# A per-layer gate stage with its weight tiles outside four rows, and the fourth norm's last rows in pairs

## The chip, the cores and the metric

The program runs on one core of a Trainium2 chip. The metric is the time of one execution in device microseconds (us); the median of the runs counts. The engines are TensorE (PE, with its weight loads as PEld), VectorE (DVE), ScalarE (ACT), GpSimd (POOL), and SyncE (SP), which only issues DMAs. Each works through its own instruction stream in order and waits on semaphores that the others raise.

## What is computed

Two transformer blocks run on a sequence of 1024 tokens of width 1024, in float32. The stage of this change is the end of the first block: a feed-forward part, then a gate computed from the normed x that scales a projection of a second input p (1024 x 256), and then the final norm, whose result is the second block's x. The second block begins with a norm of its own and with gates from `w_in_2`.

```python
x = x + jnp.square(jax.nn.relu(h @ w_ffn_up[i])) @ w_ffn_down[i]
ple_gate = jax.nn.sigmoid(rmsnorm(x, g_ple[i]) @ w_ple_gate[i])
x = x + ple_gate * (p[i] @ w_ple_proj[i])
...
x = rmsnorm(x, g_final)                  # "x2", kept for the second block's residual
h = rms_norm(x, g_mix_2); gates = sigmoid((h @ w_in_2)[..., gate columns] + b_gate_2)
```

## The kernel before

**Tiles and products.** Tokens lie in eight rows t = 0..7 of 128; rows 0-3 are half 0, rows 4-7 half 1. Every large product is made in float32 precision from halves: a value is split into a high part (ACT, a copy with rounding) and a low part (a subtraction), and `three` issues three matmuls per 128-deep slice. A weight tile is two slices of 128 x 512. It goes from HBM into one of three stage buffers (SP), ACT makes its high part (L398), and POOL (L406) or DVE (L414) its low part; in the per-layer stage the two take turns. A ring holds five split tiles. `o.released()` after a tile's last use puts the conversion of the tile five further on into the order at that place; its DMA was issued when the tile three before it was done.

**Order.** `order_*` functions write one list of steps by hand, and each engine runs its own part of every step in that order. A step that stands earlier in the list stands earlier in the queue of each engine that has a part in it. `handover` is a barrier for all engines but PE: each waits for the last signal that the others raised before it.

**Norm.** `norm(nid)` is a generator that the stages advance. For each four rows: `rstd` (small DVE operations around a square root on ACT), then per row `scale_rows` on DVE (L523), `turn` on PE (eight 128 x 128 transposes, L534), its high part on ACT (L544) and low part on DVE (L555). Two buffers `xn` hold scaled rows. Norm 3 feeds the per-layer gate, norm 4 the second block; both write the transposed `hT`.

**Last feed-forward group** (`order_ffn`, end). For t = 0..7 the two halves n = 0, 1 of a row are multiplied (6 matmuls each), added to x on DVE (L2045) and squared on ACT (L1903). From row 3 on, norm 3 of half 0 is advanced by one step a row. At row 7 each tile is released right after its last matmuls, ahead of that row's squares and of turn 3.

**Per-layer stage** (`order_first_half`). After the handover p (1 MB) and `w_ple_proj` (1 MB) are loaded. For each half and each n, four weight tiles are taken. A row's gate is 24 matmuls in a row through all four tiles (`pe_ple_gate`). It needs the turned rows of the whole half. Then come the projection (`pe_ple_proj`, four plain float32 matmuls, L2139), sigmoid on ACT (L2148), product and sum on DVE (L2162, L2165) and a square on ACT (L1903). All eight transposes-by-four of p (`p_turn`, L2102) stand after the first row's gate. At the fourth row all four tiles are released at once, ahead of that row's sigmoid. The x2 norm runs in pairs of rows (`order_rows`: root, scaling L2062, four squares L2073 on ACT). Norm 4 of half 0 is advanced in the second half.

**Start of the second block** (`order_lru`). Four gate tiles are used on half 0 each and then on half 1 each. `staggered` puts norm 4's step for rows 4-7 first, turn 4 after the third gate, turn 5 after the fourth, then turns 6 and 7.

**PSUM.** `K.open(key)` gives the eight banks in a ring ("all") and waits until the bank's last holder has been read.

Of the kernel before, what the change touches and what calls it, by code (L numbers as in the profile page):

```python
# [256 lines left out]
class Kernel:  # L257
# [26 lines left out]
    def restart(self):  # L284
        for s in self.signals():
            s.n = 0
        for q in (self.pe, self.a, self.v, self.g, self.sp):
            q.seen, q.latest = {}, None
        self.ring_at = {"all": 0, "work": 0}
        self.holder = {}  # L290
# [7 lines left out]
    def open(self, key, ring="all"):  # L298
# [4 lines left out]
        elif ring == "work":  # L303
            banks = (3 + self.ring_at["work"] % 4,)
            self.ring_at["work"] += 1
        else:
            banks = ring
# [44 lines left out]
    def need_hT(self, nid, half):  # L352
        self.pe.wait_ge(self.S.hT_hi, (nid, half))
        self.pe.wait_ge(self.S.hT_lo, (nid, half))

# [194 lines left out]
def dve_turn(K, nid, t):  # L550
    v, n = K.v, K.norms[nid]
    for k0 in range(0, ND, 4):
# [3 lines left out]
                          ALU.subtract).then_inc(*K.S.hT_lo.up((nid, t // (NT // 2))))  # L556
        K.free(("turn", nid, t, k0), K.S.hT_lo)
# [1532 lines left out]
def sp_ple_load(K):  # L2090
    io, S = K.io, K.S
    K.sp.q.dma_start(K.prow[:, :, :], io["p"][0, 0].rearrange("(t p) c -> p t c", p=P)).then_inc(*S.p_load.up("p", 16))
    K.sp.q.dma_start(K.wpp[:, :, :], io["w_ple_proj"][0].rearrange("(k p) n -> p k n", p=P)).then_inc(*S.p_load.up("p", 16))

def pe_p_turn(K):
    for c in range(2):
        for t0 in range(0, NT, 4):
            b = K.open(("pT", c, t0))
            K.pe.wait_ge(K.S.p_load, "p")  # L2100
            for t in range(4):
                mm = K.pe.q.transpose(b[:, t * P:(t + 1) * P], K.prow[:, t0 + t, c * P:(c + 1) * P], K.ident[:, :])  # L2102
            mm.then_inc(*K.S.mm.up(("pT", c, t0)))

def dve_p_turn(K):
    v, S = K.v, K.S
    for c in range(2):
        for t0 in range(0, NT, 4):
            v.wait_ge(S.mm, ("pT", c, t0))  # L2110
            v.q.tensor_copy(K.pT[:, c, t0 * P:(t0 + 4) * P], K.bank(("pT", c, t0))).then_inc(*S.dve_evac.up(("pT", c, t0)))
            K.free(("pT", c, t0), S.dve_evac)

def pe_ple_gate(K, t, n, w0):
    pe, S, key = K.pe, K.S, ("ple", t, n)
    tc, hT = slice(t * P, (t + 1) * P), K.norms[3]["hT"]
    b = K.open(key)
    K.need_hT(3, t // (NT // 2))
    k = 0  # L2120
    for w in range(w0, w0 + 4):
        K.need_weight(w)
        hi, lo = K.weight(w)
        for i in range(2):
            mm = three(pe.q, b, (hT[0][:, k, tc], hT[1][:, k, tc]), (hi[:, i, :], lo[:, i, :]), k == 0, k == ND - 1)
            k += 1
        if w == w0 + 3:
            mm.then_inc(*S.mm.up(key))
            K.tile_done(w)
        elif t % (NT // 2) == NT // 2 - 1:  # L2130
            mm.then_inc(*S.mm.up(("tile", w)))

def pe_ple_proj(K, t, n):
    b = K.open(("pp", t, n))
    K.pe.wait_ge(K.S.dve_evac, ("pT", 1, 4))
    K.pe.wait_ge(K.S.p_load, "p")
    for k in range(2):
        mm = K.pe.q.matmul(b, K.pT[:, k, t * P:(t + 1) * P], K.wpp[:, k, n * HALF:(n + 1) * HALF], start=k == 0, stop=k == 1)  # L2139
# [337 lines left out]
def lay_out(K):  # L2477
# [71 lines left out]
    for i in (1, 2):  # L2549
# [15 lines left out]
    K.act = {1: pair("act", [P, 4, S])}  # L2565
    m.lo = above_x
# [5 lines left out]
    K.pT, K.prow, K.wpp = put("pT", [P, 2, S]), put("prow", [P, NT, PLE]), put("wpp", [P, 2, D])  # L2572
# [26 lines left out]
        4: {"to": K.gain, "row": io["g_mix_2"][0], "after": (3, NT - 1)},  # L2599
# [91 lines left out]
class Order:  # L2691
# [33 lines left out]
    def norm(self, nid):  # L2725
        for half in range(NHALF):
            ts = range(half * NT // 2, (half + 1) * NT // 2)
# [361 lines left out]
def order_ffn(o, f, norm, last_group, block_done):  # L3089
# [3 lines left out]
    for kind, i in ffn_plan(blocks):  # L3093
# [31 lines left out]
def order_first_half(o):  # L3125
    io = o.io
    norm = order_merge(o, 1, 2, [(io["w_o_mla"][0], NR, False), (io["w_o_rwkv"][0], NR, True)], io["w_out"][0])
    ple_norm = o.norm(3)
# [270 lines left out]
```

## Time and profile before

| | us |
|---|---|
| median of 3 runs (3667.73 to 3674.22) | 3673.79 |
| the profiled execution, its own time | 3660.88 |
| span of the profiled execution | 3659.5 |
| PE busy | 3488.4 (95%) |
| per-layer stage, from norm 3's turn of row 3 to the first gate of half 1 in the second block | 1949.68 to 2137.84 |

### The profile page before, as it was taken

To read this page: it belongs to the slowest core of one execution; us is meant where nothing else is said; L and a number is where in the kernel's file an instruction comes from. 1 tells how busy PE (TensorE), PEld (TensorE's weight loads), DVE (VectorE), ACT (ScalarE), POOL (GpSimd) and SP (SyncE) were. 2 spreads that over 40 slices of the span, in tenths; PEclk is the share of its full clock that TensorE was granted. 3 is DMA by queue.
4 is the path that set the end of the run, shared out by engine and by line. 5 is a ranking of instruction groups with operands and counts; after the bars stand their busy time and mean duration, and the time that the engine had idled before them with its cause. 6 is when DMAs were issued, how large, how long until landed. Compare 5 with 4: busy or idle time off the path is not lost.

```text
span 3659.5 us, 48530 instructions
## 1 busy us (share of the span) xinstructions
PE 3488.4 (95%) x20382; PEld 2834.9 (77%) x20382; DVE 1776.6 (49%) x2383; ACT 1291.5 (35%) x2197; POOL 1055.1 (29%) x592
## 2 busy tenths in 40 slices
PE   6999999999989999999998989999899999999998
PEld 5788887887668788888886667777687788888886
DVE  4563636426754433333335538984544434434435
ACT  4342333334543321211223547771232333223232
POOL 3221222110023233333331116762344223223221
PEclk9999999999999999999999999999899999999999
DMA  4111111010035311111112232223454311111111
GB/s 141 33 29 45 40 31 45 27 50 13 1 110 173 98 52 50 49 52 47 46 52 75 86 98 80 79 78 98 160 186 135 124 46 49 50 47 47 52 46 52
DMA packets 282377, 253.66 MB, mean 69 GB/s; under 512 B 11621, under 2 KB 221985, under 8 KB 282160
## 3 DMA queue, kind: packets, MB, share of 16 engines
q1 hardware_dynamic: 267552, 216.29, 19.4%
q10 hardware_dynamic: 11520, 25.17, 1.8%
q0 software_dynamic: 3088, 9.10, 0.7%
q8 instruction: 162, 2.65, 0.3%
q14 instruction: 55, 0.45, 0.0%
HBM read 213.81 MB, written 36.70 MB: 68 GB/s over the span
## 4 chain that ended last, share of the span: by engine, by line

## 5 line engine op out<-in xcount | busy, mean ns | idle before, releaser
L406 POOL TENSOR_TENSOR weight_lo<-stage,weight_hi 128x1024 fp32r<-128x1024 f32 (+4 forms) x265 | 625.8, 2366 | 1439.0 <-ACT weight_hi L398 1438.8
L369 PE MATMUL psum<-hT_hi,weight_hi 128*128 128x512 f32 x2240 | 891.0, 398 | 10.1 <-DVE hT_lo L555 7.4
L370 PE MATMUL psum<-hT_lo,weight_hi 128*128 128x512 f32 x2240 | 879.3, 393 | 0.0
L371 PE MATMUL psum<-hT_hi,weight_lo 128*128 128x512 f32 x2240 | 878.8, 392 | 0.0
L369 PEld LDWEIGHTS psum<-hT_hi,weight_hi 128*128 128x128 f32 x2240 | 425.8, 190 | 109.7 <-issue 11.8
L370 PEld LDWEIGHTS psum<-hT_lo,weight_hi 128*128 128x128 f32 x2240 | 425.6, 190 | 91.7 <-issue 4.3
L371 PEld LDWEIGHTS psum<-hT_hi,weight_lo 128*128 128x128 f32 x2240 | 425.0, 190 | 90.1
L398 ACT ACTIVATE weight_hi<-stage 128x1024 fp32r<-128x1024 f32 (+4 forms) x329 | 316.0, 975 | 464.5 <-PE psum L371 411.5
L2045 DVE TENSOR_TENSOR x<-x,psum 128x512 f32<-128x512 f32 x432 | 289.8, 686 | 215.4 <-PE psum L371 214.8
L369 PE MATMUL psum<-weight_hi,act_hi 128*128 128x512 f32 x864 | 339.0, 392 | 0.0
L371 PE MATMUL psum<-weight_hi,act_lo 128*128 128x512 f32 x864 | 338.7, 392 | 0.0
L370 PE MATMUL psum<-weight_lo,act_hi 128*128 128x512 f32 x864 | 338.7, 392 | 0.0
L2006 DVE SCALAR_TENSOR_TENSOR xn<-raw,param,xn 128x1024 f32<-128x1024 f32 x44 | 104.1, 2366 | 350.2 <-ACT xn L1991 350.2
L1943 DVE TENSOR_TENSOR rel<-rel,psum 128x512 f32<-128x512 f32 x64 | 44.0, 687 | 305.4 <-ACT rel L1932 305.4
L371 PEld LDWEIGHTS psum<-weight_hi,act_lo 128*128 128x128 f32 x864 | 162.4, 188 | 36.2
L370 PEld LDWEIGHTS psum<-weight_lo,act_hi 128*128 128x128 f32 x864 | 162.4, 188 | 36.0
L369 PEld LDWEIGHTS psum<-weight_hi,act_hi 128*128 128x128 f32 x864 | 162.4, 188 | 35.9
L414 DVE TENSOR_TENSOR weight_lo<-stage,weight_hi 128x1024 fp32r<-128x1024 f32 (+2 forms) x64 | 111.6, 1750 | 125.8 <-ACT weight_hi L398 122.1
L369 PE MATMUL psum<-br_hi,weight_hi 128*128 128x512 f32 x352 | 141.0, 401 | 19.2 <-POOL br_lo L1785 12.1
L1951 POOL TENSOR_TENSOR act_lo<-rel,act_hi 128x512 fp32r<-128x512 f32 x64 | 83.3, 1301 | 238.5 <-ACT act_hi L1936 238.5
L370 PE MATMUL psum<-br_lo,weight_hi 128*128 128x512 f32 x352 | 139.9, 397 | 0.0
L371 PE MATMUL psum<-br_hi,weight_lo 128*128 128x512 f32 x352 | 139.9, 397 | 0.0
(376 smaller groups left out, 5282.4 us busy)
## 6 DMA issues: line engine op xcount, KB each, us to landing
stage<-in_w_in SPq DMA_DIRECT2D x64, 512.0 KB, 4.0
stage<-in_w_up SPq DMA_DIRECT2D x44, 512.0 KB, 3.8
scratch_gates<-gate ACTq DMA_DIRECT2D x64, 256.0 KB, 2.0
gs<-scratch_gates SPq DMA_DIRECT2D x64, 256.0 KB, 2.8
stage<-in_w_out SPq DMA_DIRECT2D x32, 512.0 KB, 4.9
stage<-in_w_ffn_up SPq DMA_DIRECT2D x32, 512.0 KB, 4.2
stage<-in_w_ffn_down SPq DMA_DIRECT2D x32, 512.0 KB, 3.6
stage<-in_w_down SPq DMA_DIRECT2D x22, 512.0 KB, 3.5
```

The source lines that it names most:

```text
L369: q.matmul(out, stat[0], mov[0], start=first, stop=False)
L370: q.matmul(out, stat[0], mov[1], start=False, stop=False)
L371: return q.matmul(out, stat[1], mov[0], start=False, stop=final)
L398: a.q.activation(hi, K.staged(w), ACT.Copy).then_inc(*S.w_hi.up(w))
L406: g.q.tensor_tensor(lo, K.staged(w), hi.bitcast(F32), ALU.subtract).then_inc(*S.w_lo_pool.up(w))
L414: v.q.tensor_tensor(lo, K.staged(w), hi.bitcast(F32), ALU.subtract).then_inc(*S.w_lo_dve.up(w))
L1943: v.q.tensor_tensor(r[:, :], r[:, :], K.bank(key), ALU.mult).then_inc(*S.dve_evac.up(key))
L1951: g.q.tensor_tensor(lo, K.rel[K.relu_order[i, h] % 3][:, :], hi.bitcast(F32), ALU.subtract).then_inc(*S.act_lo.up((f, i, h)))
L2006: v.step(v.q.scalar_tensor_tensor(cv[:, :], raw[:, 1:SEQ + 1], K.p_("conv_f_w_2", 2 * NF2 + c), cv[:, :], ALU.mult, ALU.add))
L2045: v.q.tensor_tensor(dst, dst, K.bank(key), ALU.add).then_inc(*S.x.up(("f", f, g, t, n)))
```

## The change

1. The per-layer stage loops over weight tiles outside the four rows for the first three of its four (half, n) parts: a tile is used on all four rows (their sums stay open in PSUM banks 0 to 3) and released at once. In the fourth part (half 1, n = 1) the rows are outside, with four resident tiles, and all four are released at the very end, behind the last row's steps. Each row's gate waits for its own turned row only (`need_row`).
2. p and `w_ple_proj` are loaded in halves. The first half is loaded at the start of the last feed-forward group and turned at its end, the second half is loaded after the handover and turned between the first two parts.
3. The two tiles of the last feed-forward group are released after row 7's steps.
4. Norm 3 of half 1 advances one step after each tile pass of half 0. The x2 norm takes rows 0-3 together after the second part, then rows 4-5 and 6-7. Norm 4 is grouped (0-3), (4-5), (6-7). `order_lru` advances it once ahead of each of the first four gates.
5. Turns from norm 3's half 1 on, the second half of p and the projections use banks 4 to 7 in a ring of their own.

```diff
 def pe_turn(K, nid, t):
-        b = K.open(("turn", nid, t, k0))
+        b = K.open(("turn", nid, t, k0), "upper" if nid == 4 or (nid, t // (NT // 2)) == (3, 1) else "all")
...
+def sp_ple_load(K, part):
+    if part == 0:
+        sp.wait_ge(S.act_lo, (1, NF - 1, 1))
+    sp.q.dma_start(K.prow[part][:, :, :], rows[:, part * NT // 2:(part + 1) * NT // 2, :]).then_inc(*S.p_load.up(part, 16))
+    sp.q.dma_start(K.wpp[part][:, :, :], io["w_ple_proj"][0].rearrange("(k p) n -> p k n", p=P)[:, :, part * HALF:(part + 1) * HALF]).then_inc(*S.p_load.up(part, 16))
...
+def pe_ple_gate(K, t, n, w, i):
+    b = K.open(key, (t % (NT // 2),)) if i == 0 else K.bank(key)
+    K.need_row(3, t)
+    K.need_weight(w)
+    hi, lo = K.weight(w)
+    for k in range(2):
+        mm = three(pe.q, b, [x[:, 2 * i + k, tc] for x in hT], (hi[:, k, :], lo[:, k, :]), (i, k) == (0, 0), (i, k) == (3, 1))
...
-        4: {"to": K.gain, "row": io["g_mix_2"][0], "after": (3, NT - 1)},
+        4: {"to": K.gain, "row": io["g_mix_2"][0], "after": ("rows", "x2", 0)},
...
 def order_ffn(o, f, norm, last_group, block_done):
                     o.do("down", f, i, t, n, w0 + n)
-                    if t == NT - 1:
-                        o.released()
                     o.do("down_rows", f, i, t, n)
                 block_done(t)
+            o.released(2)
...
 def order_first_half(o):
+    ple_norm, mix_norm = o.norm(3), o.norm(4, ((0, rows), (rows, rows + 2), (rows + 2, NT)))
+    def last_group():
+        o.do("gain", 3)
+        o.do("ple_load", 0)
     def block_done(t):
+        if t >= rows - 1:
             advance(ple_norm, 1)
+        if t == NT - 1:
+            o.do("p_turn", 0)
+    order_ffn(o, 1, norm, last_group, block_done)
+    o.do("ple_load", 1)
     o.do("gain", "x2")
+    for half, n in ((0, 0), (0, 1), (1, 0)):
+        w0 = tiles(n)
+        ts = range(half * rows, (half + 1) * rows)
+        for w in range(4):
             for t in ts:
+                o.do("ple_gate", t, n, w0 + w, w)
+                if w == 3:
+                    end_row(t, n)
+            o.released()
+            if half == 0:
+                advance(ple_norm, 1)
+            elif w:
+                advance(mix_norm, 1)
+        if (half, n) == (0, 0):
+            o.do("p_turn", 1)
+        if (half, n) == (0, 1):
+            order_rows(o, "x2", ts)
             o.do("gain", 4)
+    w0 = tiles(1)
+    for t in range(rows, NT):
+        for w in range(4):
+            o.do("ple_gate", t, 1, w0 + w, w)
+        end_row(t, 1)
+        if t % 2:
+            order_rows(o, "x2", (t - 1, t))
+        advance(mix_norm, 1)
+    o.released(4)
...
 def order_lru(o, mix_norm):
-    staggered([block(c) for c in range(GATES_AHEAD)], mix_norm, 3)
+    blocks = [block(c) for c in range(GATES_AHEAD)]
+    for n, b in enumerate(blocks):
+        advance(mix_norm, 1)
+        next(b)
+    finish(mix_norm)
+    for b in blocks:
+        finish(b)
```

`end_row` is the projection and the mix of one row; `tiles` takes the four tiles of one n. `lay_out` places the first halves of p and `w_ple_proj` where the last feed-forward group leaves room.

## Rows read from the trace of the kernel before

**Rows 1.** The page's busy times: engine, us, share of the span.

```profile
PE 3488.4 (95%) x20382; PEld 2834.9 (77%) x20382; DVE 1776.6 (49%) x2383; ACT 1291.5 (35%) x2197; POOL 1055.1 (29%) x592
```

**Rows 2.** Two stretches: us, engines' busy time, granted PE clock, DMA share, GB/s.

```profile
1960.00:1980.00 20.00, 14.13 (x49) 10.16 (x48) 5.02 (x12) 4.83 (x7) 0.00 (x0) 0.74 0.27 99
...
2140.00:2160.00 20.00, 20.00 (x82) 16.32 (x82) 0.00 (x0) 5.25 (x6) 5.44 (x3) 0.91 0.29 92
```

**Rows 3.** Timeline of PE: start, us, line, operands, count, idle before and its cause.

```profile
1949.68 1.03 PE L534 MATMUL psum<-ident,xn 128*128 128x128 f32 x8
...
1954.88 0.47 PE L369 MATMUL psum<-weight_hi,hT_hi 128*128 128x512 f32 x1 [4.16 <-POOL weight_lo L406]
...
1967.17 3.65 PE L2102 MATMUL psum<-ident,prow 128*128 128x128 f32 x16 [4.99 <-DMA wpp<-in_w_ple_proj]
...
1976.38 0.39 PE L369 MATMUL psum<-weight_hi,hT_hi 128*128 128x512 f32 x1
...
1981.18 1.88 PE L2139 MATMUL psum<-wpp,pT 128*128 128x512 f32 x4
...
2020.65 1.88 PE L2139 MATMUL psum<-wpp,pT 128*128 128x512 f32 x4
...
2027.86 1.88 PE L2139 MATMUL psum<-wpp,pT 128*128 128x512 f32 x4
...
2034.75 0.77 PE L369 MATMUL psum<-weight_hi,hT_hi 128*128 128x512 f32 x1 [3.62 <-POOL weight_lo L406]
...
2040.29 1.88 PE L2139 MATMUL psum<-wpp,pT 128*128 128x512 f32 x4
...
2088.34 1.88 PE L2139 MATMUL psum<-wpp,pT 128*128 128x512 f32 x4
...
2096.41 1.88 PE L2139 MATMUL psum<-wpp,pT 128*128 128x512 f32 x4
...
2122.19 1.94 PE L534 MATMUL psum<-ident,xn 128*128 128x128 f32 x8 [7.52 <-DVE xn L523]
...
2137.84 0.77 PE L369 MATMUL psum<-hT_hi,weight_hi 128*128 128x512 f32 x1 [1.67 <-DVE hT_lo L555]
```

**Rows 4.** Timelines of POOL, ACT and DVE at the end of the feed-forward part.

```profile
1950.15 4.65 POOL L406 TENSOR_TENSOR weight_lo<-stage,weight_hi 128x1024 fp32r<-128x1024 f32 x2 [22.78 <-ACT weight_hi L398]
...
1952.77 1.06 ACT L544 ACTIVATE hT_hi<-psum 128x512 fp32r<-128x512 f32 x2
...
1953.37 1.29 DVE L555 TENSOR_TENSOR hT_lo<-psum,hT_hi 128x512 fp32r<-128x512 f32 x2 [2.23 <-ACT hT_hi L544]
```

**Rows 5.** ACT: two sigmoids one after the other in the chain of one row.

```profile
2051.07 0.60 ACT L2148 ACTIVATE sg<-psum 128x512 f32<-128x512 f32 x1
...
2053.78 0.58 ACT L2148 ACTIVATE sg<-psum 128x512 f32<-128x512 f32 x1
```

**Rows 6.** ACT and DVE: x2 norm of two rows behind the projection of 2020.65.

```profile
2024.83 1.28 ACT L481 ACT_TABLE_LOAD   x1
...
2027.35 2.48 DVE L2062 SCALAR_TENSOR_TENSOR x<-x,squares,gain 128x1024 f32<-128x1024 f32 x2
...
2030.53 0.61 ACT L2073 ACTIVATE junk<-x 128x512 f32<-128x512 f32 x1
```

**Rows 7.** ACT and DVE: conversion of four tiles released together.

```profile
2099.80 2.94 ACT L398 ACTIVATE weight_hi<-stage 128x1024 fp32r<-128x1024 f32 x3
...
2101.82 2.60 DVE L414 TENSOR_TENSOR weight_lo<-stage,weight_hi 128x1024 fp32r<-128x1024 f32 x1 [3.33 <-ACT weight_hi L398]
...
2108.50 1.23 DVE L414 TENSOR_TENSOR weight_lo<-stage,weight_hi 128x1024 fp32r<-128x1024 f32 x1 [4.09 <-ACT weight_hi L398]
```

**Rows 8.** DVE and POOL: a scaled row while POOL converts.

```profile
2061.82 3.43 DVE L523 SCALAR_TENSOR_TENSOR xn<-x,squares,gain 128x1024 f32<-128x1024 f32 x1
...
2061.81 5.67 POOL L406 TENSOR_TENSOR weight_lo<-stage,weight_hi 128x1024 fp32r<-128x1024 f32 x2 [23.38 <-ACT weight_hi L398]
```

**Rows 9.** A DMA issue: engine, KB, us from issue to landing.

```profile
wpp<-in_w_ple_proj SPq DMA_DIRECT2D x1, 1024.0 KB, 11.3
```

More of the change, by code:

```diff
@@ L288, in restart @@
             q.seen, q.latest = {}, None
-        self.ring_at = {"all": 0, "work": 0}
+        self.ring_at = {"all": 0, "work": 0, "upper": 0}
         self.holder = {}
@@ L305, in open @@
             self.ring_at["work"] += 1
+        elif ring == "upper":
+            banks = (4 + self.ring_at["upper"] % 4,)
+            self.ring_at["upper"] += 1
         else:
@@ L2106, in dve_p_turn, with pe_p_turn @@
-def dve_p_turn(K):
+def sp_ple_load(K, part):
+    io, S, sp = K.io, K.S, K.sp
+    rows = io["p"][0, 0].rearrange("(t p) c -> p t c", p=P)
+    if part == 0:
+        sp.wait_ge(S.act_lo, (1, NF - 1, 1))
+    sp.q.dma_start(K.prow[part][:, :, :], rows[:, part * NT // 2:(part + 1) * NT // 2, :]).then_inc(*S.p_load.up(part, 16))
+    sp.q.dma_start(K.wpp[part][:, :, :], io["w_ple_proj"][0].rearrange("(k p) n -> p k n", p=P)[:, :, part * HALF:(part + 1) * HALF]).then_inc(*S.p_load.up(part, 16))
+def pe_p_turn(K, half):
+    for c in range(2):
+        b = K.open(("pT", c, half), "upper" if half else "all")
+        K.pe.wait_ge(K.S.p_load, half)
+        for t in range(NT // 2):
+            mm = K.pe.q.transpose(b[:, t * P:(t + 1) * P], K.prow[half][:, t, c * P:(c + 1) * P], K.ident[:, :])
+        mm.then_inc(*K.S.mm.up(("pT", c, half)))
@@ L2107, in dve_p_turn @@
+def dve_p_turn(K, half):
     v, S = K.v, K.S
+    v.wait_ge(S.act_lo, (1, NF - 1, 1))
     for c in range(2):
[L2109 to L2115, printed above, removed]
+        v.wait_ge(S.mm, ("pT", c, half))
+        v.q.tensor_copy(K.pT[half][c][:, :], K.bank(("pT", c, half))).then_inc(*S.dve_evac.up(("pT", c, half)))
+        K.free(("pT", c, half), S.dve_evac)
@@ L2565, in lay_out @@
     K.act = {1: pair("act", [P, 4, S])}
+    act_end = m.lo
     m.lo = above_x
@@ L2723, in released, with norm @@
             self.slot(self.slot_of[self.back - 1])
-    def norm(self, nid):
-        for half in range(NHALF):
-            ts = range(half * NT // 2, (half + 1) * NT // 2)
+    def norm(self, nid, groups=((0, NT // 2), (NT // 2, NT))):
+        for group in groups:
+            ts = range(*group)
             self.do("rstd", nid, ts)
@@ L3125, in order_first_half @@
 def order_first_half(o):
-    io = o.io
+    io, rows = o.io, NT // NHALF
     norm = order_merge(o, 1, 2, [(io["w_o_mla"][0], NR, False), (io["w_o_rwkv"][0], NR, True)], io["w_out"][0])
-    ple_norm = o.norm(3)
+    ple_norm, mix_norm = o.norm(3), o.norm(4, ((0, rows), (rows, rows + 2), (rows + 2, NT)))
+    def last_group():
+        o.do("gain", 3)
+        o.do("ple_load", 0)
     def block_done(t):
-        if t >= NT // NHALF - 1:
+        if t >= rows - 1:
             advance(ple_norm, 1)
-    order_ffn(o, 1, norm, lambda: o.do("gain", 3), block_done)
@@ L3134, in order_first_half, with tiles @@
-    o.do("ple_load")
+        if t == NT - 1:
+            o.do("p_turn", 0)
+    order_ffn(o, 1, norm, last_group, block_done)
+    o.do("ple_load", 1)
     o.do("gain", "x2")
-    mix_norm, first = None, True
     o.engines = ["G", "V"]
-    for half in range(NHALF):
-        ts = range(half * NT // 2, (half + 1) * NT // 2)
-        for n in range(2):
-            w0 = o.take(*rows512(o.io["w_ple_gate"][0], n))
-            for t in ts:
-                o.do("ple_gate", t, n, w0)
-                if t == ts[-1]:
-                    o.released(4)
-                if first:
-                    o.do("p_turn")
-                    first = False
-                o.do("ple_proj", t, n)
-                o.do("ple_mix", t, n)
-                if mix_norm is None:
-                    advance(ple_norm, 0 if (t, n) == (1, 0) else 1)
-                elif 2 <= n * (NT // 2) + t - NT // 2 < 2 + NORM_STEPS:
-                    advance(mix_norm, 1)
-                if n and t % (NT // 2) == 2:
-                    order_rows(o, "x2", (t - 2, t - 1))
-        order_rows(o, "x2", (ts[-1] - 1, ts[-1]))
-        if half == 0:
-            o.do("gain", 4)
-            mix_norm = o.norm(4)
+    def tiles(n):
+        return o.take(*rows512(io["w_ple_gate"][0], n))
```

56 lines of the change are left out of this document (27 added, 29 removed).

## The prediction

> **What bounds the kernel now.** I read the page's busy times first: PE is busy for 95% of the span [rows 1], so PE time or PE waits must go if the end is to come earlier. The change adds and removes no matmul; only waits of PE and stretches at half clock can move. So I took PE's timeline from turn 3 to the first gate of half 1 in the second block, and for each gap the ACT, DVE and POOL timelines ahead of it. First the undisturbed price of each piece [rows 3]. The last 21 matmuls of a gate run from 1976.38 to 1981.18, 0.228 us each, so a pass of one tile over four rows, or a whole gate (24 matmuls), is 5.47. From one projection to the next without a turn is 7.21 (2020.65 to 2027.86), so a projection is 1.74. With a turn it is 8.07 (2088.34 to 2096.41), so a turn is 0.86, and p's sixteen transposes are about 1.72 at full clock.
>
> Against these prices the stage loses, before the last projection ends (2096.41 + 1.74 = 2098.15):
> - (a) First gate. From turn 3 (1949.68) to the gate (1954.88) is 5.20 for 0.86 of work: 4.3. The bracket blames POOL, but the low part of turn 3 ended at 1954.66 [rows 4], and the gate needs it. The gate then lasts until 1962.18 (1967.17 less its 4.99) instead of 5.6 us: 1.7. Sum 6.0.
> - (b) p. PE waits 4.99 for the DMA; from 1967.17 to the next projection but one (1981.18) is 14.0 instead of 1.7 + 7.2. The granted clock of that stretch is 0.74, part of it at 1.2 GHz [rows 2]. Sum 10.1.
> - (c) The second half's first tiles are released and converted four at once: 3.62 for POOL's low part, and 2027.86 to 2040.29 is 12.43 instead of 7.21 [rows 3]. Sum 5.2.
> - (d) Total: 1949.68 to 2098.15 is 148.5; the work is 16 x 7.21 + 9 x 0.86 + 1.7 = 124.8. That leaves 23.7, so 2.4 beyond a to c, mostly norm 4's turn 0.
>
> Behind it is the tail, 2098.15 to 2137.84 = 39.7, with 7.5 of waiting for turn 4 [rows 3]. The clock is 0.91 from 2140 to 2160 [rows 2] and low from 2137.84: some 2.9 more. Tail 42.6.
>
> **The change part by part.** I call the four parts' tiles A, B, C, D and the gate tiles G.
>
> *What goes.* (a) A gate now needs its own row, so row 0 starts right behind turn 3 and p's first half: 1949.68 + 0.86 + 0.86 = 1951.4. Row 3 is needed 3 x 1.37 later, at 1955.5; its high part leaves the queue place behind two weight conversions, so it is no later than before (1954.66). All 6.0 go. (b) The first loads of p (two DMAs, 1 MB) are issued by SP behind the second release of the group before, some 22 us (16 x 6 x 0.228) ahead of the turn; the slower DMA of twice that took 11.3 [rows 9]. Nothing on SP behind them is urgent: the tiles queued there are used after 1970. They share the DMA with norm 3's gain row on POOL's queue, which has 10 us. POOL's low part and DVE's two copies have 16 us until the first projection. The second halves follow the handover and have some 20 us. All 10.1 go. (c) One tile is released every 5.5 us against one conversion (ACT 1.0, POOL 2.3 [rows 4] or DVE 1.23 [rows 7]). All 5.2 go. With (d)'s 2.4 this is 23.7. The later release in `order_ffn` also runs in the second block's last group, where no tile is left to convert: nothing. Norm 4's gain waits on POOL for the first x2 row (Q + 7.7 in the count below), with no conversion behind it before Q + 13.8 and its user at Q + 19: nothing. PSUM costs nothing: bank 3 is wanted again 4 us after the last projection of a part, and the chain sigmoid to square takes 2.7 [rows 5] against 3.1 per row of PE.
>
> *New wait at turn 4 of norm 3.* Its root step stands behind the handover, and the handover behind the two tiles released late: turn 3's high part ends near 1953.0, two copies on ACT, two on POOL at 2.33 [rows 4] until 1958.8. Then B's next tile on ACT (1.0), root and five small operations (1.3), and a scaling, 1.24 alone to 3.43 under POOL [rows 6, 8]: 1963.5, as POOL is half through. PE wants the turn at 1951.4 + 2 x 5.47 = 1962.3. Cost 1.2, between 0 and 3.
>
> *New wait at turn 0 of norm 4.* From the end Q of the last projection of part two: square done Q + 2.4 (table load at 2024.83 against the projection of 2020.65 [rows 6]); D's first tile on ACT and DVE, then rows 0-3: first store from Q + 6.5, four at 1.24 to 11.5, squares 1.3 later to 12.8. Now ACT makes two released D tiles (2.0: 14.8), DVE the second one's low part beside POOL (2.60 [rows 7]: 17.4), root 1.75, and the scaling meets POOL on the third tile, the pattern of [rows 8]: 3.43, to Q + 22.6. PE is there after three passes, Q + 16.4. Wait 6.2 (0 to 8; the lower end is rows 0-3 not held by conversions), and some 2 for the clock, as in (a). Cost 8.2.
>
> *Tail.* From the end E5 of row 5's projection. x2 squares of rows 4-5 end at +8.8 (2030.53 + 0.61 against 2020.65 + 1.74 [rows 3, 6]); turn 3's copy 1.06, table load 1.28, sigmoid to square of row 6 to +14.0; another table load and root for rows 4-5, scaling to +17.8; row 7's mix waits for these on ACT and DVE, square +20.0; rows 6-7 stored at +25.0; row 5 scaled +26.2. PE's last projection ends at +15.3 (0.86 + 2 x 7.21), so turn 4 waits 2.6 and turn 5 stands at the end of the projection + 11.1. Then ACT converts the four tiles released last: 9.9 as in [rows 7] (2099.80 to 2109.73), one behind a DMA. The handover ends at 22.0. Behind it on ACT are turn 5's copy, a sigmoid with its store, two table loads, and the root: scaled row 6 at 29.6. PE: turn 5 and two gates, slow at first, to 25.2; wait 4.5; turn 6, gate, turn 7, gate, with 2 for the clock: 44.5. Against 42.6 this costs 1.9 (-2 to 8).
>
> **Sum.** -23.7 + 1.2 + 8.2 + 1.9 = -12.4. Profiled: 3660.9 - 12.4 = 3648.5. The span lies 1.4 under its own time, and that execution 12.9 under the median; executions scatter by 6. From the median: 3673.8 - 12.4 = 3661.4.
>
> The Trainium skill bears on the chains of turn 0 and of the tail. In [rows 6] a table load of 1.28 (2024.83 to 2026.11) is followed within 1.24 by the root, five small operations and the first scaling, so nothing else is in it. "ScalarE: Activation LUTs", section "What ACT_TABLE_LOAD costs", has a drain of about 1380 ns on top of a load of 1283 ns at every switch of the set. It would speak against splitting the norm into pairs: seven switches stand on the tail's chain, an estimated 9.7 us more by the page, and the gain would shrink to 2.7. The trace disagrees with the drain and agrees with the load.
>
> **The rivals.**
> - *Most of it is given back* (0.25). Turn 0 waits 10 with its clock, turn 4 waits 3, the tail costs 7: 23.7 - 20 = 4 gained, 3670. For it: each chain is serial on two in-order queues. Against it: each piece has a row. The drain at table switches belongs here; the rows give it no more than 0.02 of this.
> - *The chains hide* (0.17). If rows 0-3 are through before the conversions reach ACT, turn 0 waits 0 to 1 and the rest as summed: 20 gained, 3654. Against it: the order puts both D tiles ahead of the root.
> - *Slower: DVE becomes the bound of the passes* (0.08). POOL now converts during passes instead of in four bursts. If every pass met a contended scaling (3.43), two low parts of a turn (1.29 [rows 4]) and a contended conversion (3.40 at most, by the ratio in rows 8), DVE would need 8.1 against PE's 6.3. From 6.3 on each turn waits; six turns lie in passes, 1.8 and 2 of clock each: 23, and 3673.8 - 12.4 + 23 = 3684. Against it: POOL and DVE take tiles in turn, so a pass has one or the other: 4.7 or 3.8.
> - *The early load comes late*: the turn of p would wait as before; 22 us against 11 leave 0.01 for it, within the first rival.
>
> **How the numbers follow.** The forecast has 0.50 (8 to 17 gained), the rivals 0.25, 0.17 and 0.08. Range: from 20 gained with 2 of scatter (3652) to 2 gained (3672), leaving out the slower case and the edges. A measurement of this kernel can tell some 0.2% (7 us) from no change: faster 0.67, same 0.25, slower 0.08.
>
> **What would show it.** Right: no PE wait on p or on POOL's weights between turn 3 and the second part; a wait of about 6 at norm 4's turn 0 and of 8 ahead of turn 5; the second part's end near 2015 (1951.4 + 8 x 7.21 + 5 x 0.86 + 1.2). Wrong: a wait at every turn (third rival), none at turn 0 (second), a stage loss before the last projection above 15 (first).

## The result, and the profile after

The changed kernel takes 3652.73 us (median of 4 runs, 3649.94 to 3655.81) against 3670.76 (4 runs, 3664.99 to 3674.22) for the kernel before: a ratio of 0.9950 [0.9933, 0.9966], 18.0 us less. Five more runs (a1 below) gave 3655.9 against 3669.23, a ratio of 0.9962 [0.9949, 0.9976], 13.3 us less. The forecast was 12.4 us less.

The page's busy times come first. PE has the same count of instructions and the same work as in [rows 1]:

```profile
PE 3490.0 (95%) x20382; PEld 2838.1 (78%) x20382; DVE 1773.4 (49%) x2383; ACT 1289.7 (35%) x2195; POOL 1055.7 (29%) x592
```

So only waits of PE and its clock have moved. Two stretches of the changed kernel (us, engines' busy time, granted PE clock, DMA share, GB/s) are those of [rows 2], where the clock was 0.74 and 0.91:

```profile
1960.00:1980.00 20.00, 18.25 (x86) 14.35 (x85) 10.47 (x16) 6.98 (x10) 9.10 (x5) 1.00 0.52 185
...
2140.00:2160.00 20.00, 20.00 (x90) 16.57 (x89) 0.47 (x3) 5.70 (x7) 9.57 (x4) 1.00 0.41 129
```

PE's timeline of the changed kernel, from turn 3 of norm 3 to the first gate of half 1 in the second block (start, us, line, operands, count, idle before and its cause). Line 542 is the turn (534 before), 2114 the turn of p, 2152 the projection. Put beside [rows 3], the waits for POOL's weights and for the DMA of p are gone. A wait of 1.75 for a scaled row at turn 4 of norm 3 is new, and the one at turn 0 of norm 4 is 5.66, where it was 1.61 in the kernel before (its line is the first below; the rest is the changed kernel).

```profile
2065.39 1.06 PE L534 MATMUL psum<-ident,xn 128*128 128x128 f32 x8 [1.61 <-DVE xn L523]
...
1955.08 1.03 PE L542 MATMUL psum<-ident,xn 128*128 128x128 f32 x8
1955.95 1.04 PE L2114 MATMUL psum<-ident,prow 128*128 128x128 f32 x8
...
1969.63 1.06 PE L542 MATMUL psum<-ident,xn 128*128 128x128 f32 x8 [1.75 <-DVE xn L531]
...
2018.98 1.88 PE L2152 MATMUL psum<-wpp,pT 128*128 128x512 f32 x4
...
2042.87 1.94 PE L542 MATMUL psum<-ident,xn 128*128 128x128 f32 x8 [5.66 <-DVE xn L531]
...
2087.57 1.88 PE L2152 MATMUL psum<-wpp,pT 128*128 128x512 f32 x4
...
2091.92 1.07 PE L542 MATMUL psum<-ident,xn 128*128 128x128 f32 x8 [2.48 <-DVE xn L531]
...
2100.21 1.94 PE L542 MATMUL psum<-ident,xn 128*128 128x128 f32 x8 [7.23 <-DVE xn L531]
...
2118.47 1.94 PE L542 MATMUL psum<-ident,xn 128*128 128x128 f32 x8 [4.28 <-DVE xn L531]
...
2126.29 1.03 PE L542 MATMUL psum<-ident,xn 128*128 128x128 f32 x8
...
2132.65 0.39 PE L377 MATMUL psum<-hT_hi,weight_hi 128*128 128x512 f32 x1
```

The stage is measured on this timeline in two pieces: from turn 3 to the end of the last projection (its start + 1.74), and from there to the first gate of half 1, the tail. The experiments below use the same two.

| us | before | changed | difference |
|---|---|---|---|
| turn 3 to the end of the last projection | 148.5 | 134.2 | -14.2 |
| tail | 39.7 + 2.7 of clock behind it | 43.3, no clock lost behind it | +0.9 |
| stage | 190.9 | 177.6 | -13.3 |

The clock behind the tail is counted from the trace: in the kernel before the 13 matmuls from 2137.84 to 2143.50 take 5.66 where 13 x 0.227 is 2.95, so 2.7 (the prediction has 2.9).

The profiled executions themselves differ by only 5.1 us (3660.88 and 3655.81). The changed one came 5.4 later to turn 3 (1955.08 against 1949.68). Of this, 1.6 is slow clock behind turn 0 of norm 3 (last section). The other 3.8 lie ahead of that turn, in work that the change leaves alone but for p's early load. That load does not explain them: a4 below, which loads p later, starts the stage at 1953.20, and c3, which loads it early, at 1953.05. In all, the eleven other profiles, in the experiments below, start it between 1953.05 and 1960.51. The profiled execution of the kernel before was 9.9 under its median, the changed one 3.1 over its own. So the stage is compared by its own length, and the whole by medians.

### The profile page after: what moved, and what is told of

It reads as the page before. It is cut to its first block, busy times and chain, and to the rows that moved or that the text cites. A ratio compares the mean times of both kernels' runs of the same rounds, so it can differ in the third digit from the quotient of the medians.

```text
span 3654.5 us, 48533 instructions
## 1 busy us (share of the span) xinstructions
PE 3490.0 (95%) x20382; PEld 2838.1 (78%) x20382; DVE 1773.4 (49%) x2383; ACT 1289.7 (35%) x2195; POOL 1055.7 (29%) x592
## 4 chain that ended last, share of the span: by engine, by line
```

## Experiments

Each kernel is the changed one with the edit shown; for c1 the edit is shown against a3, for c2 against b4. "To the last projection" and "tail" are the two pieces above, from one profile each; the median and the ratio to the kernel before are from the runs.

| kernel | to the last projection | tail | median | ratio |
|---|---|---|---|---|
| changed | 134.2 | 43.3 | 3652.73 | 0.9950 [0.9933, 0.9966] |
| a1 the same again | 136.9 | 43.7 | 3655.9 | 0.9962 [0.9949, 0.9976] |
| a2 no pairs | 135.2 | 39.0 + some 2.3 of clock | 3657.43 | 0.9969 [0.9957, 0.9981] |
| a3 rows outside | 148.5 | 45.6 | 3670.34 | 1.0005 [0.9996, 1.0014] |
| a4 load late | 136.3 | 43.3 | 3657.68 | 0.9971 [0.9962, 0.9980] |
| b1 norm first | 128.7 | 45.4 | 3651.73 | 0.9954 [0.9939, 0.9968] |
| b2 conversions late | 135.1 | 39.1 | 3651.7 | 0.9962 [0.9946, 0.9979] |
| b3 early release | 133.0 | 45.8 | 3654.34 | 0.9964 [0.9953, 0.9975] |
| b4 all three | 127.2 | 38.1 | 3642.83 | 0.9931 [0.9917, 0.9944] |
| c1 rows outside, early release | 137.9 | 45.0 | 3659.85 | 0.9980 [0.9969, 0.9990] |
| c2 gate ahead of turn 5 | 127.2 | 37.0 | 3640.45 | 0.9931 [0.9918, 0.9943] |
| c3 b4 again | 127.2 | 38.1 | 3642.58 | 0.9931 [0.9919, 0.9944] |

The kernel before: 148.5, 42.4, and medians of 3669.23 (a), 3668.26 (b) and 3668.86 (c) beside these runs.

**a1: the changed kernel again.** The question was whether 18 or 12 is its gain.

> The changed kernel once more, against the kernel before on the same chip. My theory: the per-layer stage and the tail behind it are worth 13.5 us by the two profiles (from norm 3's turn of row 3 to the first gate of half 1: 188.2 and 2.9 of slow clock before, 177.6 after), and the rest of the 18 us between the medians is scatter: the ratio comes out near 0.9963. The rival: something outside the stage gives another 4 to 5 us: the ratio stays at 0.995.

This result puts the gain at 13 to 14 (1 - 0.9962 of 3669 is 13.9), as the theory has it, and its interval (0.9949 to 0.9976) just includes the rival's 0.995. So that the first 18 held scatter is likely and not shown. Most waits are those of the first profile within 0.3; ahead of turn 5 it was 6.35 instead of 7.23. Yet the piece to the last projection is 2.7 longer. Of this 1.6 is slow clock behind turn 4 of norm 3 (7.99 from it to turn 5, 6.40 in the first profile) and 0.7 clock behind turn 0 of norm 4. By a1's profile the stage is 180.6, 10.3 shorter than before. One profile of a kernel tells a piece to no better than some 3 us, and differences below are to be read with that.

**a2: norm 4 without pairs.** Rows 4-7 are scaled as one group of four, behind all of the stage, and its turns are staggered over the gates as before.

```diff
-    ple_norm, mix_norm = o.norm(3), o.norm(4, ((0, rows), (rows, rows + 2), (rows + 2, NT)))
+    ple_norm, mix_norm = o.norm(3), o.norm(4)
...
-        advance(mix_norm, 1)
+        if t < rows + 2:
+            advance(mix_norm, 1)
...
-    blocks = [block(c) for c in range(GATES_AHEAD)]
-    for n, b in enumerate(blocks):
-        advance(mix_norm, 1)
-        next(b)
...
+    staggered([block(c) for c in range(GATES_AHEAD)], mix_norm, 3)
```

> Norm 4 in two groups of four rows again, with the second block's start in the order of before (the step for rows 4-7 first, turn 4 after the third gate, turn 5 after the fourth, then 6 and 7); all else as changed. Theory of the prediction: the tail's length is the chain behind the handover on ACT and DVE, not PE's order, so pairs buy little: the last row's sigmoid no longer waits for the root step of rows 4-5 (2 us earlier), the handover ends 3 us earlier, the gates of PE fill the wait, and the tail from the last projection to the first gate of half 1 falls from 43.3 to 36 to 38 us: 5 to 7 us faster than the changed kernel. Rival, what the pairs are for: without them all four turns come behind one late root step, as before, and the tail grows by 4 to 8 us.

The expectation failed. PE of this kernel no longer waits for pairs of rows, but for POOL's low part of the second gate's tile, then for the last turn:

```profile
2105.54 0.77 PE L377 MATMUL psum<-hT_hi,weight_hi 128*128 128x512 f32 x1 [6.73 <-POOL weight_lo L414]
...
2129.29 1.35 PE L542 MATMUL psum<-ident,xn 128*128 128x128 f32 x8 [2.64 <-DVE xn L531]
...
2132.15 0.76 PE L377 MATMUL psum<-hT_hi,weight_hi 128*128 128x512 f32 x1 [1.50 <-DVE hT_lo L563]
```

The tiles are released only behind the last row's steps, so there is nothing split that PE could use while it waits. The tail is 41.3 with the clock, 2 shorter than the changed kernel's and longer than the 36 to 38 expected; it did not grow by 4 to 8 either, as the rival has it. The total is the same as a1's within the intervals. In this order pairs win nothing that these runs can show. No run has groups of four together with the spread releases of b2.

**a3: rows outside the tiles again** in the first three parts, four tiles released together behind the last row's steps. The early load of p and the wait for each row's own turn stay.

```diff
-        for w in range(4):
-            for t in ts:
+        for t in ts:
+            for w in range(4):
                 o.do("ple_gate", t, n, w0 + w, w)
-                if w == 3:
-                    end_row(t, n)
-            o.released()
+            end_row(t, n)
+            if t == ts[-1]:
+                o.released(4)
             if half == 0:
                 advance(ple_norm, 1)
-            elif w:
+            elif t > ts[0]:
                 advance(mix_norm, 1)
```

> The first three parts with the rows outside and the four tiles released together behind the fourth row's steps, as the fourth part has it; p's early load, banks, norm groups as changed. Theory: the order of passes is what removes the wait for tiles: two to three waits of 3 to 4 us with 1 to 2 of clock each come back at the part borders (10 to 14), while the wait at norm 4's turn 0 (5.7 and 2 of clock) goes, since rows 0-3 get 7 us more: 3 to 7 us slower than the changed kernel. Rival: tiles are no bound and only the early p and the row-wise wait matter: within 2 us, or faster by turn 0's 7.

It was 14 slower than a1, more than expected, and no different from the kernel before. PE of this kernel waits for a burst of conversions behind the first tile of the second, third and fourth part, and turn 0 of norm 4 still waits:

```profile
1998.93 0.47 PE L377 MATMUL psum<-weight_hi,hT_hi 128*128 128x512 f32 x1 [2.66 <-POOL weight_lo L414]
...
2037.03 0.55 PE L377 MATMUL psum<-weight_hi,hT_hi 128*128 128x512 f32 x1 [4.40 <-POOL weight_lo L414]
...
2061.61 1.94 PE L542 MATMUL psum<-ident,xn 128*128 128x128 f32 x8 [2.49 <-DVE xn L531]
...
2077.09 0.47 PE L377 MATMUL psum<-weight_hi,hT_hi 128*128 128x512 f32 x1 [3.53 <-POOL weight_lo L414]
```

Either the loop order or the late release could be behind that; c1 separates them.

**c1: rows outside, but the four tiles released right after their last matmuls**, ahead of the last row's projection and mix:

```diff
                 o.do("ple_gate", t, n, w0 + w, w)
+            if t == ts[-1]:
+                o.released(4)
             end_row(t, n)
-            if t == ts[-1]:
-                o.released(4)
```

> The first three parts with the rows outside again, but the four tiles of a part released ahead of the fourth row's projection, sigmoid and sums, as in the kernel before; p's early load, the row-wise wait, banks and norm groups as changed. It tells what the release place added to the loss of the run with the rows outside. Theory: that run lost 14 us because its releases stood behind the row's whole chain at each border; with the early release the early p (10) and the row-wise wait (6) show without the order of passes, less the one wait for tiles of the kernel before (5): 6 to 12 us faster than the kernel before. Rival: the order of passes is what makes room for p, norm 3 and the tiles together: within 5 us of the kernel before.

To the last projection it takes 137.9, so 10.5 of a3's 148.5 came from the place of the release alone. The kernel before releases at the same place as c1. Against it, c1 keeps 10.5 of the change's 14.2 (the change's gain is 11.6 by a1's profile). The long waits that are left are for a bank that the last product still reads, and for turn 0; the longest wait for a tile is 0.47:

```profile
1992.15 0.81 PE L2114 MATMUL psum<-ident,prow 128*128 128x128 f32 x4 [3.84 <-DVE sg L2175]
...
2050.31 1.74 PE L542 MATMUL psum<-ident,xn 128*128 128x128 f32 x8 [4.64 <-DVE xn L531]
```

In the total it gains 7 to 9 (a ratio of 0.9980, and 3659.85 against 3668.86), where the changed kernel gains 13 to 14. So what c1 shares with the changed kernel (the early p, the row-wise wait, the banks, the grouping of the norms) carries more than half of the gain; no run separates these. What is left for the tile-outside order is 1 to 4 us by the profiles, and the interval of c1's ratio overlaps a1's.

**a4: both halves of p loaded behind the handover**, the first turned after the third tile pass instead of after turn 3 (a semaphore for each half).

```diff
         o.do("gain", 3)
-        o.do("ple_load", 0)
...
-        if t == NT - 1:
-            o.do("p_turn", 0)
...
+    o.do("ple_load", 0)
     o.do("ple_load", 1)
...
+            if (half, n, w) == (0, 0, 2):
+                o.do("p_turn", 0)
```

> Both halves of p and of its weights loaded after the handover, the first half turned after the third tile pass, ahead of the first projection, each half with a semaphore of its own; all else as changed. Theory: the order of passes alone gives p 16 us of cover, so the early load is not needed: within 2 us of the changed kernel, PE's wait for p at most 1 us. Rival: the early load is what removed the 10 us: 5 us or more slower than the changed kernel, with a PE wait on the load.

PE of this kernel waits 0.33 for a bank at the start and 1.18 for p's copies, a little more than expected:

```profile
1954.56 0.50 PE L377 MATMUL psum<-weight_hi,hT_hi 128*128 128x512 f32 x1 [0.33 <-ACT psum L1912]
...
1978.45 1.95 PE L2152 MATMUL psum<-wpp,pT 128*128 128x512 f32 x4 [1.18 <-DVE pT L2123]
```

The total is 1.8 above a1's, within the intervals. With tiles outside the load need not be early: three passes over four rows (16.4 us of matmuls) cover it, because the tile-outside order wants p only in the fourth pass.

**b1: norm 4's first step ahead of the release after the first pass of the third part**, so the two conversions stand behind the root on ACT, and DVE's one of them behind the first scaling.

```diff
-            o.released()
             if half == 0:
+                o.released()
                 advance(ple_norm, 1)
-            elif w:
+            elif w == 0:
                 advance(mix_norm, 1)
+                o.released()
+            elif w:
+                o.released()
+                advance(mix_norm, 1 if w > 1 else 0)
```

> The changed kernel, but norm 4's first step (root of rows 0-3, scaling of row 0) stands ahead of the release behind the third part's first tile pass, not behind the release of its second; the turns stay where they are. Theory: PE's wait of 5.66 at norm 4's turn 0, with 2 of slow clock, is a queue effect: two weight copies on ACT, one low part on DVE beside POOL and a scaling held by POOL stand ahead of or across the step. With the step first the scaled row is there 36.2 to 38.3 - 20.7 = 15.5 to 17.6 after the projection, PE comes at 16.2: wait 0 to 1.5, full clock, 5 to 8 us faster than the changed kernel. Rival: the wait is the length of the x2 norm itself (root, four stores, eight squares), which no order of the queues shortens: the wait stays above 3 and the time within 2 us.

Turn 0 waits 1.42 instead of 5.66 and keeps its clock. These are DVE's scaling, POOL's conversion and PE's turn 0 in this kernel, and behind them ACT's fourth tile and PE's turn 6 in the tail:

```profile
2036.30 2.53 DVE L531 SCALAR_TENSOR_TENSOR xn<-x,squares,gain 128x1024 f32<-128x1024 f32 x1 [0.98 <-DMA gain<-in_g_mix]
2035.36 2.39 POOL L414 TENSOR_TENSOR weight_lo<-stage,weight_hi 128x1024 fp32r<-128x1024 f32 x1 [5.97 <-ACT weight_hi L406]
2038.98 1.06 PE L542 MATMUL psum<-ident,xn 128*128 128x128 f32 x8 [1.42 <-DVE xn L531]
...
2104.99 1.06 ACT L406 ACTIVATE weight_hi<-stage 128x1024 fp32r<-128x1024 f32 x1 [6.47 <-DMA stage<-in_w_in]
...
2114.82 1.94 PE L542 MATMUL psum<-ident,xn 128*128 128x128 f32 x8 [6.73 <-DVE xn L531]
```

The piece to the last projection fell to 128.7, 5.5 less than in the changed kernel: 4.2 of wait and the clock. The tail gave 2.1 of it back: the DMA of the fourth tile kept ACT for 6.47 instead of 4.57, and turn 6 waited 6.73 instead of 4.28. So the wait went as expected, while of the 5 to 8 us the profile shows 3.5 in both pieces together, and the total can't be told from the changed kernel's two results.

**b2: the tail's conversions moved.** One of the four tiles is released at the end of the stage, and one ahead of each of gates 2 to 4, behind norm 4's next step.

```diff
-    o.released(4)
+    o.released()
...
         advance(mix_norm, 1)
+        if n:
+            o.released()
         next(b)
```

> The changed kernel, but of the four tiles of the fourth part only one is released ahead of the handover, and one each ahead of the second, third and fourth gate of the second block. Theory: the tail is set by the handover, which waits for four conversions (9.9 us, one behind a DMA): with one it ends 6 us earlier, row 6 is scaled before PE comes to turn 6, the wait of 4.3 and its slow clock go, and the tail from the last projection to the first gate of half 1 falls from 43.3 to 37 to 39: 4 to 7 us faster than the changed kernel. The wait of 7.2 at turn 5 stays, since it stands ahead of the handover. Rival: the conversions only move behind the handover and delay the sigmoids, whose banks the turns need: the wait moves to turn 6 or 7 and the tail stays above 42.

The tail is 39.1 instead of 43.3. PE's waits at turn 6 and at its gate are down to

```profile
2116.86 0.66 PE L542 MATMUL psum<-ident,xn 128*128 128x128 f32 x4 [0.34 <-ACT gate L648]
...
2117.93 0.47 PE L377 MATMUL psum<-hT_hi,weight_hi 128*128 128x512 f32 x1 [0.42 <-POOL weight_lo L414]
```

That is the mechanism that was expected. The piece to the last projection was 0.9 longer here, and in the total b2 can't be told from the changed kernel's two results either.

**b3: the feed-forward part's last two tiles released as in the kernel before**, each right after its last matmuls.

```diff
                     o.do("down", f, i, t, n, w0 + n)
+                    if t == NT - 1:
+                        o.released()
...
-            o.released(2)
```

> The changed kernel with the last feed-forward group's two tiles released right behind their last matmuls, as before the change. Theory: the later release costs the wait of 1.75 at norm 3's turn 4, through the handover: the two low parts on POOL end some 3.5 us earlier, the root step follows, and POOL no longer holds a 0.16 us operation of it for 2 us; wait 0 to 0.5, 1 to 2 us faster, too little for the timing to tell. Rival: row 3's high part comes later and the first pass waits 1 us for it: same.

Turn 4 of norm 3 waits 0.58 instead of 1.75, 1.2 less, and the piece to the last projection is 1.2 shorter. One part of the theory failed: POOL still holds the small operation (L496), for 2.16. These are PE's turn, POOL's tile and the operation on DVE in this kernel:

```profile
1973.90 1.07 PE L542 MATMUL psum<-ident,xn 128*128 128x128 f32 x8 [0.58 <-DVE xn L531]
...
1969.42 2.38 POOL L414 TENSOR_TENSOR weight_lo<-stage,weight_hi 128x1024 fp32r<-128x1024 f32 x1 [1.79 <-ACT weight_hi L406]
...
1969.67 2.16 DVE L496 TENSOR_TENSOR squares<-squares 128x4 f32<-128x4 f32 x1
```

Its tail (45.8) again had the late DMA: ACT waited 6.15 for the fourth tile. In the total this small edit can't be told from a1.

**b4: b1, b2 and b3 together, and c3, the same once more.**

> The three edits together: norm 4's first step ahead of the release, conversions of the last four tiles spread over the second block's first gates, the feed-forward group's tiles released early. Theory: the three waits lie one behind the other on PE, so their gains add: 10 to 16 us faster than the changed kernel, ratio to the kernel before near 0.9925. Rival: a chain that ran beside PE with a margin becomes the next bound and takes half of it back: 5 to 8 us.

> The three edits together once more, to compare with on the same chip: ratio to the kernel before 0.992 to 0.9945, and 8 to 15 us under the changed kernel's two results.

To the last projection 127.2 in both (7.0 less than the changed kernel), tail 38.1 in both (5.2 less): 12.3 together. The medians, 3642.83 and 3642.58, stand at 0.9931 twice, 10 to 13 us under the changed kernel's two medians. The slowest of these eleven runs (3649.68) is under the fastest of the changed kernel's nine (3649.94): a version that beats both. The longest waits left are those ahead of turns 4 and 5 of norm 4, 2.47 and 7.23.

**c2: b4 with the first gate ahead of turn 5**, to fill that 7.23; the ring of banks is moved on by two for it.

```diff
-        advance(mix_norm, 1)
         if n:
+            advance(mix_norm, 1)
             o.released()
         next(b)
+        if n == 0:
+            advance(mix_norm, 1)
```

> The three edits together as in the run before, and the second block's first gate ahead of turn 5, in a bank that is free (the ring is moved on by two banks), so that PE has 5.5 us of work in the wait of 7.2. Theory: the tail is the chain squares, one conversion, handover, sigmoid, root, scaling on ACT, DVE and POOL, and PE's work only fills it: the second gate then waits 3 to 4 us for its tile, and the tail falls by 1 to 2 us of the 5.5. Rival: PE's order was the bound: the tail falls by 5 us or more.

The wait ahead of turn 5 went to 0.15, but PE of this kernel then waited for the second gate's tile:

```profile
2094.22 1.06 PE L542 MATMUL psum<-ident,xn 128*128 128x128 f32 x8 [0.15 <-DVE xn L531]
...
2098.76 0.77 PE L377 MATMUL psum<-hT_hi,weight_hi 128*128 128x512 f32 x1 [3.47 <-POOL weight_lo L414]
```

The tail is 37.0 against 38.1, and the totals can't be told apart (0.9931 each). So PE's order was not the bound: work put into the wait only moves it to the next split tile. The tail is set by the chain on ACT, DVE and POOL.

## Why the prediction was right

**The sum.** Forecast: -23.7 + 1.2 + 8.2 = -14.3 to the last projection, +1.9 in the tail, -12.4. Measured: -14.2, +0.9, -13.3 in the profile, -11.6, +1.3, -10.3 in a1's, and -13 to -18 by medians. The measured 3652.73 lies only 0.7 above the lower end of the range (3652) and nearer to the second rival's 3654 than to the forecast's 3661.4. Of the 8.7 between, 3.0 is the kernel before, whose median is 3670.76 here instead of 3673.79, and 5.6 a gain of 18.0 instead of 12.4. a1's 13.3 suggests that some of this is scatter, so that the figure stayed inside the range is in part luck. What bears out the forecast is the waits, piece by piece.

**What goes.** All of (a), (b) and (c) went: the price of the pieces is 124.8, the changed kernel's is 134.2, and the 9.4 left are the waits of 1.75 and 5.66 and a rest of 2.0. Of this rest 1.7 is the clock at turn 0: from it to the next projection (2046.82) is 3.95 for 0.86 of turn and 1.37 of matmuls. There is no wait for p or for a weight tile in this stretch, as "what would show it" asked; the second part ends at 2020.72, 65.6 behind turn 3 (forecast 64.9 by its sum, "near 2015"). That (a) went is read from this timeline; no run takes the row-wise wait away by itself.

The sizes of (b) and (c) came out, but not their reasons. For (b) I had named the early load; a4 shows that with tiles outside it is not what counts, since p is then wanted only in the fourth pass. For (c) I had blamed four conversions at once. The rows speak against it: the kernel before also converts four at once between its first two parts, and there projection follows projection by 8.07 (1996.45 to 2004.52), the price with a turn and no wait. Ahead of its third part the x2 step of rows 0 and 1 [rows 6] stands in front of the copies on ACT. The copies started at 2031.14, 3.3 after the part's last gate had ended (2027.86). In c1, with the same release of four at once but the x2 step behind it, ACT copies from 2019.03, 3.1 before that gate ends (2022.17), and no wait for a tile follows. First the kernel before, then c1:

```profile
2031.14 2.93 ACT L398 ACTIVATE weight_hi<-stage 128x1024 fp32r<-128x1024 f32 x3
...
2019.03 3.10 ACT L406 ACTIVATE weight_hi<-stage 128x1024 fp32r<-128x1024 f32 x3
```

So (c) was a matter of what stands ahead of the conversions, and not of their number. No run moves the x2 step alone. a3 and c1 show the same thing from the other side: with rows outside, a release behind the last row's steps costs 10.5.

**Turn 4 of norm 3.** Forecast 1.2, measured 1.75, and the step that made it was another one. POOL, ACT and DVE of the changed kernel ahead of that turn:

```profile
1959.02 4.75 POOL L414 TENSOR_TENSOR weight_lo<-stage,weight_hi 128x1024 fp32r<-128x1024 f32 x2 [27.86 <-ACT weight_hi L406]
1965.16 2.38 POOL L414 TENSOR_TENSOR weight_lo<-stage,weight_hi 128x1024 fp32r<-128x1024 f32 x1 [0.24 <-ACT weight_hi L406]
1964.02 1.06 ACT L406 ACTIVATE weight_hi<-stage 128x1024 fp32r<-128x1024 f32 x1 [4.14 <-POOL weight_lo L414]
1965.42 2.15 DVE L496 TENSOR_TENSOR squares<-squares 128x4 f32<-128x4 f32 x1
1968.20 1.28 DVE L531 SCALAR_TENSOR_TENSOR xn<-x,squares,gain 128x1024 f32<-128x1024 f32 x1
```

ACT stands 4.14 at the handover until POOL has its two tiles, as forecast. But I let the scaling (L531) meet POOL's third tile; it met nothing (1.28). A small operation of the root step (L496, 128 x 4, 0.16 elsewhere) took 2.15, up to the end of POOL's tile (1965.16 + 2.38 = 1967.54). So that the wait came out near the forecast is in part luck: I had counted some 1.2 of hold on the scaling, and 2.0 fell on L496. b3, with the two tiles released earlier, takes 1.2 of the wait away, so the release behind row 7's steps caused that much. The hold on L496 is still there in b3. Without it the scaled row would be ready some 2.0 earlier, more than the 0.58 that is left; this is an estimate, no run removes the hold.

**Turn 0 of norm 4.** Forecast 6.2 and 2 for the clock, measured 5.66 and 1.7. From Q = 2018.98 + 1.74 = 2020.72, on ACT, DVE and POOL of the changed kernel:

```profile
2026.90 4.87 DVE L2071 SCALAR_TENSOR_TENSOR x<-x,squares,gain 128x1024 f32<-128x1024 f32 x4
...
2033.15 2.00 ACT L406 ACTIVATE weight_hi<-stage 128x1024 fp32r<-128x1024 f32 x2
2034.28 2.40 POOL L414 TENSOR_TENSOR weight_lo<-stage,weight_hi 128x1024 fp32r<-128x1024 f32 x1 [5.23 <-ACT weight_hi L406]
2035.17 2.59 DVE L422 TENSOR_TENSOR weight_lo<-stage,weight_hi 128x1024 fp32r<-128x1024 f32 x1 [3.40 <-ACT weight_hi L406]
...
2039.31 2.34 POOL L414 TENSOR_TENSOR weight_lo<-stage,weight_hi 128x1024 fp32r<-128x1024 f32 x1 [2.63 <-ACT weight_hi L406]
2039.32 4.60 DVE L531 SCALAR_TENSOR_TENSOR xn<-x,squares,gain 128x1024 f32<-128x1024 f32 x2
```

The x2 squares are through and ACT takes the two tiles at Q + 12.4 (forecast 12.8), they are split on ACT at Q + 14.4 (14.8), DVE's low part ends at Q + 17.0 (17.4), and the turn starts at Q + 22.15 (22.6). The scaling did meet POOL here: two take 4.60 instead of 2.48. b1 is the test of the cause: with the conversions behind the norm's step 4.2 of the wait goes, and the clock stays up. The 1.42 that stays has its own causes, a gain row that lands 0.98 late and a scaling of 2.53 beside POOL.

**Tail.** From the end of the last projection, 2089.31: turn 4 waits 2.48 (forecast 2.6), turn 5 starts at +10.9 (11.1) behind a wait of 7.23 (about 8), and turn 6 at +29.2 (29.7), the first gate of half 1 at +43.3 (44.5). The end of the handover shows on ACT:

```profile
2101.13 2.94 ACT L406 ACTIVATE weight_hi<-stage 128x1024 fp32r<-128x1024 f32 x3
...
2108.64 1.06 ACT L406 ACTIVATE weight_hi<-stage 128x1024 fp32r<-128x1024 f32 x1 [4.57 <-DMA stage<-in_w_in]
2111.04 1.09 ACT L552 ACTIVATE hT_hi<-psum 128x512 fp32r<-128x512 f32 x2 [1.34 <-DVE weight_lo L422]
```

at +21.7 (forecast 22.0). Of the 1.2 that the tail is shorter than forecast, 0.5 is there at turn 6 already, and the rest is clock behind it: 14.2 to the gate, forecast 12.7 + 2. b2 shows the cause of the wait at turn 6: the four conversions ahead of the handover; moved, the tail is 4.2 shorter.

**The rivals.** Most given back: no, the losses to the last projection are 9.4, far under its 15. The chains hide: no, turn 0 waited. DVE as the bound of the passes: no, two turns wait in that stretch and not six, and DVE is busy for 10.47 of the 20 us from 1960 to 1980. The drain at table switches, which would have spoken against the pairs, is not there in the changed kernel either: ACT of that kernel ends a table load at 2087.96 + 1.28 = 2089.24 and starts the root at 2089.26:

```profile
2087.96 1.28 ACT L489 ACT_TABLE_LOAD   x1
2089.26 0.20 ACT L489 ACTIVATE squares<-squares 128x2 f32<-128x2 f32 x1
```

Where "ScalarE: Activation LUTs" of the Trainium skill ("What ACT_TABLE_LOAD costs") adds about 1380 ns of drain to a load, this trace has 0.02. That pairs did not pay in the total either (a2) needs another reason; a2's rows point to the late release (6.73 for a tile), which no run tests with groups of four.

What stays open: why the stage starts between 1953 and 1960 in these profiles, and whether the one profile of the kernel before, at 1949.68, is only an early one.

## What to carry to other kernels

In a stage whose engines run in-order queues, look first at where the conversion of the next weight tiles stands in the order, not only at how many there are: the place of a release ahead of or behind a row's small steps was worth 10.5 us between a3 and c1, and three such moves gave another 12 in the profile. The steps of the chain that PE waits for (a norm's root, a scaling) belong ahead of a conversion that nobody wants yet. Price a chain by adding the durations of its steps from the profile, each under the load that runs beside it, and compare the stage's own length: executions of one kernel scatter here by about as much as the effect. Take that length from more than one profile: two of the changed kernel differ by 3.

## What was not expected of the hardware

**A DVE operation with both operands in SBUF is held while POOL's runs, not slowed.** The operation of 128 x 4 at 1965.42 took 2.15 instead of 0.16, and ended at 1967.57, 0.03 after POOL's tile. The conversion at 2035.17 ended 1.08 after POOL's (2036.68), and the scaling of b1 at 2036.30 ended 1.08 after POOL's (2037.75). This fits what the Trainium skill says in "SBUF — State Buffer", section "SBUF: two separate sides": the port pair that DVE and GpSimd share is an exclusive lock for a whole instruction, for a DVE operation with two SBUF inputs too, and the loser blocks. I had counted it from [rows 7, 8], for scalings and conversions alone, and partly by a ratio (3.40 for a conversion in the third rival; 2.59 is measured). It holds for the smallest operation as well, at a price set by POOL's. An operation with one operand from PSUM is not held: in the changed kernel two low parts of a turn took 1.29 inside POOL's tile, as they do alone:

```profile
1977.43 2.38 POOL L414 TENSOR_TENSOR weight_lo<-stage,weight_hi 128x1024 fp32r<-128x1024 f32 x1 [9.88 <-ACT weight_hi L406]
...
1977.87 1.29 DVE L563 TENSOR_TENSOR hT_lo<-psum,hT_hi 128x512 fp32r<-128x512 f32 x2 [3.66 <-ACT hT_hi L552]
```

**The same load lands at different times.** ACT waited for the fourth tile of the tail 4.57 (changed), 4.60 (a4), 4.67 (a2), 4.79 (a1), 5.90 (c1), 6.15 (b3), 6.37 (a3) and 6.47 (b1). The load was issued 2.37 to 2.43 after POOL began its first tile in all of them. From the issue to ACT's copy it is 3.97 in the changed kernel and 5.85 in b1. The tails of the kernels with pairs follow: 43.3 to 43.7 with a wait of 4.6 to 4.8, and 45.0 to 45.8 with one of 5.9 to 6.5. Why the load takes longer in some profiles stays open.

**The clock after a wait is not the same in all executions.** After an idle of 1.97 to 1.98 ahead of turn 0 of norm 3, the next turns came 3.66 to 3.68 later in the kernel before (1938.79 to 1942.45), in a1 and in b1, and 5.25 to 5.30 later in the changed kernel (1942.57 to 1947.82) and in the nine other profiles. From 1940 to 1950 the granted clock was 1.00 in the kernel before and in a1, and 0.83 in the changed kernel and in b4, a mean of stretches at 2.4 and at 1.2 GHz.
